# Returning expert rows to their tokens by 0/1 products instead of a scatter and a read-back

## The reference

```
combine = g_onehot[..., None] * within[..., None, :] * g_w[..., None, None]   # two entries per token
hg  = einsum('sd,edf->sef', xs, w_gate)
hu  = einsum('sd,edf->sef', xs, w_up)
act = silu(hg) * hu * cw[..., None]
out = einsum('sef,efd->sd', act, w_down)
x   = x + g_f[:, None, :] * out
```

## Time and profile before

| | us |
|---|---|
| median of 3 runs | 1921.35 (1921.19 to 1922.46) |
| span of the profiled execution | 1919.5 |
| PE / DVE / ACT / POOL busy | 1742.8 / 1019.5 / 553.4 / 859.7 |
| expert stage, first gather to last addition to the residual | 485 to 772.5 |

### The profile page before, as it was taken

One profiled execution on the slowest core, in us unless ns is written; L12 is line 12 of the kernel. 1 busy time (PEld: TensorE's weight loads), 2 busy tenths in 40 slices (PEclk: granted clock), 3 DMA queues, 4 the chain that ended last, 5 costly groups with the idle time before them and its releaser, 6 DMA issues.

```text
span 1919.5 us, 27022 instructions
## 1 busy us (share of the span) xinstructions
PE 1742.8 (91%) x10840; PEld 1275.8 (66%) x10840; DVE 1019.5 (53%) x1386; ACT 553.4 (29%) x995; POOL 859.7 (45%) x408
## 2 busy tenths in 40 slices
PE   6999888999797775899989899999999899999997
PEld 4868658875332322588767667777777678888885
DVE  6586896654111002496867958665798832222112
ACT  4341461533222222334434334564100120100000
POOL 0421235441110113045252342424898968787884
PEclk8999989999798897999999999999999999999999
DMA  8821223445799997222222121213457223233331
GB/s 303 318 89 55 66 87 115 158 155 186 270 410 409 409 408 283 82 88 88 66 66 66 58 74 56 72 61 121 143 208 257 99 77 99 89 98 95 103 99 66
DMA packets 81765, 290.53 MB, mean 151 GB/s; under 512 B 11120, under 2 KB 11120, under 8 KB 81008
## 3 DMA queue, kind: packets, MB, share of 16 engines
q1 hardware_dynamic: 74880, 271.54, 40.1%
q10 hardware_dynamic: 2160, 8.91, 1.2%
q0 software_dynamic: 4608, 8.40, 1.2%
HBM read 282.25 MB, written 14.94 MB: 155 GB/s over the span
## 4 chain that ended last, share of the span: by engine, by line
PE 51%; issue 18%; POOL 13%; DMA 6%; DVE 6%; ACT 3%; SPq 2%; POOLq 0%; DVEq 0%; ACTq 0%
PE bank L2715 50%; POOL lo_ring L2658 6%; DMA arena<-weights_dram 5%; POOL hi_ring L2686 4%; POOL lo_ring L2688 3%; SPq L2992 2%; PE bank L2719 1%; DVE arena L2305 1%; DMA arena<-h_dram,slot_table 0%; DVE hT L2618 0%; DMA late<-mod_weights_dram 0%; DVE arena L2376 0%; DMA xT<-x_dram 0%; DVE arena L1154 0%; DVE xT L1169 0%
## 5 line engine op out<-in xcount | busy, mean ns | idle before, releaser
L2715 PE MATMUL bank<-h_lo,hi_ring 128*128 128x512 f32 x648 | 257.1, 397 | 0.0
L2658 POOL TENSOR_TENSOR lo_ring<-ring,hi_ring 128x1024 fp32r<-128x1024 f32 x52 | 149.9, 2886 | 234.9 <-ACT hi_ring L2652 234.9
L2715 PE MATMUL bank<-arena 64*64 64x64 f32 (+4 forms) x1880 | 207.7, 366 | 49.0 <-DMA arena<-weights_dram 39.5
L2715 PE MATMUL bank<-mix_h_hi,lo_ring 128*128 128x512 f32 x576 | 230.7, 401 | 0.0
L2688 POOL TENSOR_TENSOR lo_ring<-ring,hi_ring 128x1024 fp32r<-128x1024 f32 x77 | 208.7, 2711 | 6.0
L2715 PEld LDWEIGHTS bank<-arena 64*64 64x64 f32 (+2 forms) x1880 | 107.0, 155 | 134.5 <-issue 121.5
L2686 POOL TENSOR_TENSOR hi_ring<-ring,col 128x1024 fp32r<-128x1024 f32 x77 | 159.2, 2068 | 55.7 <-PE bank L2715 55.3
L2715 PE MATMUL bank<-mix_h_hi,hi_ring 128*128 128x512 f32 x416 | 168.3, 405 | 16.9 <-POOL lo_ring L2658 6.4
L2305 DVE SCALAR_TENSOR_TENSOR arena<-bank,col,arena 128x511 f32<-128x511 f32 (+14 forms) x240 | 156.5, 723 | 0.0
L2715 PEld LDWEIGHTS bank<-h_lo,hi_ring 128*128 128x128 f32 x648 | 123.2, 190 | 27.9
L2715 PE MATMUL bank<-ffn_h_hi,lo_ring 128*128 128x512 f32 x352 | 139.2, 395 | 0.0
(11 more groups left out here) (445 smaller groups left out, 3911.6 us busy)
## 6 DMA issues: line engine op xcount, KB each, us to landing
ring<-weights_dram SPq DMA_DIRECT2D x230, 512.0 KB, 3.6
arena<-weights_dram SPq DMA_DIRECT2D x128, 512.0 KB, 13.4
arena<-mod_weights_dram SPq DMA_DIRECT2D x54, 512.0 KB, 4.7
late<-mod_weights_dram SPq DMA_DIRECT2D x42, 512.0 KB, 3.6
hT<-weights_dram SPq DMA_DIRECT2D x20, 512.0 KB, 15.5
late<-weights_dram SPq DMA_DIRECT2D x15, 512.0 KB, 14.7
arena<-y_dram ACTq DMA_DIRECT2D x8, 512.0 KB, 7.2
con<-weights_dram SPq DMA_DIRECT2D x5, 512.0 KB, 16.4
```

Source lines behind the costliest of these rows:

```text
L2658: pool.tensor_tensor(ring_r[:, u % RING, :], ring[:, u % RING, :], hi_unit(u).bitcast(F32), ALU.subtract).then_inc(S("split"), 1)
L2715: return pe.matmul(out, lhsT, rhs, start=start, stop=stop, skip_group_check=True)
```

## The change

It replaces the way back. Each slot gets two more numbers, its token's number and its weight (`slot_token`, `slot_weight`), made by a second set of small products from the table of picks. A slot that is empty has the number of no token.

- ScalarE writes the down result times the slot's weight in fp32r (`y_up`), VectorE the remainder (`y_low`).
- VectorE compares the slot's token number with the row of 512 token numbers: a 0/1 matrix of 128 slots by 512 tokens (`token_pick`).
- PE multiplies: for each of the 8 output tiles, `y_up` and `y_low` times `token_pick`, two fp32r products 128x512 into one bank. The result lies feature-major already.
- VectorE adds it, times the gate of the block, to the residual, tile by tile, for every pair (`add_rows`).

The scatter, `y_dram`, the read-back, the scaling and adding of choices and the 32 transposes are gone. The products of pair p-1 stand in four groups between the parts of gate_up(p+1), in banks 1 and 7 in turn. Bank 1 is no longer used by turn_rows, whose two halves both go through bank 0 and stand ahead of and between the two halves of down. The last two pairs use all eight banks and are added together at the end. The loops on ACT and DVE are written out. Of the five early upper parts, one now stands ahead of the last weighted rows, two behind them, one behind the squares and one behind the norm's halves.

```diff
-            def turn_rows(p):
+            def turn_rows(p, i):
...
-                    pe.wait_ge(*at_count("expert_in", p * 2))
+                if p == 1:
+                    pe.wait_ge(*at_count("expert_in", i + 1))
+                elif p:
+                    pe.wait_ge(*at_count("expert_in", p * 2 + i))
+                into = bank[i if p < 2 else 0]
...
+            def to_tokens(p, n, start=True, stop=True):
+
+                into = token_bank(p, n)
+                if n % 4 == 0:
+                    pe.wait_ge(*at_count("token_pick", p + 1))
+                    pe.wait_ge(*at_count("y_low", p * 2 + n // 4 + 1))
+                if p < PAIRS - 2 and p * KD + n > 1:
+                    pe.wait_ge(*at_count("x_added", p * KD + n - 1))
+                d = slice(n * P, n * P + P)
+                mm(into[:, :], y_up_r[:, p % 2, d], token_pick_r[:, p % 2, :], start, False)
+                last = mm(into[:, :], y_low_r[:, p % 2, d], token_pick_r[:, p % 2, :], False, stop)
+                if stop:
+                    last.then_inc(S("in_tokens"), 1)
...
+            for p in range(PAIRS):
+                if p + 1 < PAIRS:
+                    pe.wait_ge(*at_count("expert_in", p * 2 + 4))
+                    for j in range(4):
+                        gate_up_part(p + 1, j)
+                        if p:
+                            to_tokens(p - 1, 2 * j)
+                            to_tokens(p - 1, 2 * j + 1)
+                turn_act(p)
+                if p + 2 < PAIRS:
+                    turn_rows(p + 2, 0)
...
+                if p == PAIRS - 1:
+                    pe.wait_ge(*at_count("x_added", KD * (PAIRS - 2)))
+                    pe.wait_ge(*at_count("y_low", 2 * (PAIRS - 1)))
+                    for n in (0, 1, 2, 3, 6, 7):
+                        to_tokens(p - 1, n, True, False)
+                down_half(p, w, 0)
                 if p + 2 < PAIRS:
-                    turn_rows(p + 2)
-                down(p)
...
+                    turn_rows(p + 2, 1)
+                down_half(p, w, 1)
+            for n in range(KD):
+                pe.wait_ge(*at_count("y_low", 2 * PAIRS - 1 + n // 4))
+                if n in (4, 5):
+                    to_tokens(PAIRS - 2, n, True, False)
+                to_tokens(PAIRS - 1, n, False, True)
...
+            def rows_up(p):
...
+                    act.activation(y_up_r[:, p % 2, d], bank[4 + half][:, :], ACT.Identity, bias=column("zero"),
+                                   scale=slot_weight[:, p:p + 1]).then_inc(S("y_up"), 1)
...
+                dve.tensor_scalar(token_pick_r[:, p % 2, :], token_ids, slot_token[:, p:p + 1], None, ALU.is_equal).then_inc(S("token_pick"), 1)
...
+                    dve.scalar_tensor_tensor(y_low_r[:, p % 2, d], bank[4 + half][:, :], slot_weight[:, p:p + 1], y_up_r[:, p % 2, d].bitcast(F32),
+                                             ALU.mult, ALU.subtract).then_inc(S("y_low"), 1)
...
-                pool.indirect_dma_start(out=y_d, out_offset=bass.IndirectOffsetOnAxis(ap=slot_table[:, PAIRS + p:PAIRS + p + 1], axis=0),
-                                        in_=y_rows[:, p % 2, :], in_offset=None, bounds_check=2 * T - 1, oob_is_err=False).then_inc(S(f"y_stored{p % 2}"), 16)
```

More of the change, by code:

```diff
@@ L243 @@
     "act_turned": ("combine_turned", 0),
-    "sparse_y": ("y_lo", 7),
+    "y_low": ("y_lo", 7),
     "expert_in": ("y_hi", 8),
@@ L250 @@
     "two_heads": ("totals", 1),
-    "y_picked": ("gates_lo", 1),
 }
@@ L1377, in pe_moe @@
             last.then_inc(S("ranks_done"), 1)
-            out = take(("slots",), ("slots", 1))
+            out = take(("slots",), ("slot_weights", 1))
             pe.wait_ge(*at_count("picks_ranked", 1))
@@ L1382, in pe_moe @@
                     half = slice(CAP_E * i, CAP_E * i + CAP_E)
-                    last = mm(out[half, 0:2 * PAIRS].rearrange("p (v e) -> p v e", v=2), slot_of[:, n, :],
-                              slot_value[:, :, n, i:NE:2], n == 0, n == 2 * TT - 1)
+                    last = mm(out[half, 0:PAIRS], slot_of[:, n, :], slot_value[:, 0, n, i:NE:2], n == 0, n == 2 * TT - 1)
             last.then_inc(S("slots_done"), 1)
+            pe.wait_ge(*at_count("pick_weights", 1))
+            for n in range(2 * TT):
+                for i in range(2):
+                    half = slice(CAP_E * i, CAP_E * i + CAP_E)
+                    last = mm(out[half, PAIRS:2 * PAIRS], slot_of[:, n, :], slot_value[:, 1, n, i:NE:2], n == 0, n == 2 * TT - 1)
+            last.then_inc(S("slot_weights_done"), 1)
             u0 = at["moe_units"] = unit[0]
@@ L1651, in gate_up @@
[L1651 to L1663 removed]
+            def turn_rows(p, i):
+                if i == 0:
+                    pe.wait_ge(*at_count(f"gathered{p % 2}", p // 2 * 16 + 16))
+                if p == 1:
[3 more added lines that the diff above has]
+                into = bank[i if p < 2 else 0]
+                for n in range(4):
+                    last = flip(into[:, n * P:n * P + P], rows_in[:, p % 2, (4 * i + n) * P:(4 * i + n + 1) * P])
+                last.then_inc(S("rows_turned"), 1)
@@ new lines, in gate_up_part @@
+            def gate_up_part(p, j):
+                w = [weights(p, 2 * j + e) for e in range(2)]
+                for kk in range(2):
+                    k = 2 * j + kk
+                    for e in range(2):
+                        slots = slice(CAP_E * e, CAP_E * e + CAP_E)
+                        last = mm(bank[2 + 4 * (p % 2)][slots, :], rows_t[:, p % 2, k * P + CAP_E * e:k * P + CAP_E * e + CAP_E],
+                                  w[e][:, kk * 512:kk * 512 + 512], k == 0, k == KD - 1)
+                        if kk:
+                            last.then_inc(S("unit_done"), 1)
@@ L1670, in turn_act, with down_half @@
                 last.then_inc(S("act_turned"), 1)
-            def down(p):
+            def down_half(p, w, half):
+                if p:
+                    pe.wait_ge(*at_count("y_low", p * 2 + (half - 1)))
+                for i in range(4):
+                    f, e = divmod(i, 2)
+                    last = mm(bank[4 + half][CAP_E * e:CAP_E * e + CAP_E, :], sparse_act[:, f * P + CAP_E * e:f * P + CAP_E * e + CAP_E],
+                              w[i][:, half * 512:half * 512 + 512], f == 0, f == 1)
+                    if half:
+                        last.then_inc(S("unit_done"), 1)
+                if not half:
+                    last.then_inc(S("sparse_down"), 1)
@@ L1724, in act_out @@
                 act.activation(sparse_act, bank[3][:, 0:2 * P], ACT.Copy).then_inc(S("sparse_act"), 1)
-            rows_out(0, 0)
-            rows_out(1, 1)
-            silu(0, 0, 8)
-            with act.Fori(0, PAIRS // 2 - 1) as i:
-                for j in range(2):
-                    p = i * 2 + j
-                    act_out(p)
-                    silu(p + 1, 1 - j, i * (2 * PAIR_UNITS) + (16 + PAIR_UNITS * j))
-                    rows_out(p + 2, j)
-            act_out(PAIRS - 2)
@@ new lines, in act_sparse @@
+            act.wait_ge(*at_count("slot_weights", 1))
+            rows_out(0)
+            rows_out(1)
+            silu(0)
+            for p in range(PAIRS):
+                act_out(p)
+                if p + 1 < PAIRS:
+                    silu(p + 1)
+                else:
+                    act.preload_act_table_set(LN_EXP)
+                if p + 2 < PAIRS:
+                    rows_out(p + 2)
+                if p == PAIRS - 1:
+                    act.wait_ge(*at_count("unit_done", MIX_FIRST - 4))
+                    act_upper(act, MIX_FIRST)
+                rows_up(p)
```

194 lines of the change are left out of this document (79 added, 115 removed).

## The result

The changed kernel takes 1928.7 us (median of 6 runs, 1924.6 to 1931.6) against 1921.3 us for the kernel before (6 runs on the same chip). The ratio is 1.0031 with a 95% interval of 1.0018 to 1.0044. So it is slower by 0.3 to 0.4%, some 6 to 7 us, which is more than the 0.2% that a measurement can tell. I had forecast 1923.0, within a range of 1909 to 1935. The profiled execution spans 1929.4 us, that of before 1919.5.

What follows compares the result with a forecast made beforehand. Before, the matrix engine bound first, then DMA; after, the matrix engine at 17.01 us a pair. Profiled span 1919.5 + 1.7 later + 1.85 around it = 1923.0 us; eight-in-ten range 1909 to 1935.

Steps and rivals of the forecast that it cites:

- The sign: Whole kernel against the one before: faster (below 1917.5 us) 0.30, same 0.33, slower (above 1925.2 us) 0.37.
- What binds the stage: Expert stage: the matrix engine binds at 17.0 us a pair, borders included, DMA below it; 1923.0 us, chance 0.50.
- hidden borders (1904): Expert stage: the matrix engine's queue largely hides tile-form borders; 15.65 us a pair, 1904 us in total; chance 0.24.
- DMA as the bound: Expert stage: DMA stays the bound at 16.25 us a pair, 1912.5 us in total; chance 0.04.
- the late hand-over chain: Before first products: row copies, weighted rows, remainder late, matrix engine waits; 0.65 us a pair, 1932 us; chance 0.22.
- The period: Matrix engine per pair: 11.43 existing work + 3.70 products + 1.62 borders + 0.26 copy stall = 17.01 us.
- The estimate of what DMA allows (15.65 us): Expert stage: DMA alone, without the scatters, allows 15.65 us a pair, from 16.25 us less 0.6 us.
- rival 4: Expert stage: DMA keeps binding at 16.25 us a pair, only if borders are hidden too; 1912.5 us, chance 0.04.
- The start of the stage: Before the first pair: slot-weight products and copies run beside the gather at no cost; stage taken 0.7 us earlier.
- The other half of the step: Pair 1's turns wait for only half of pair 0's row copies; gate/up starts some 0.9 us earlier, taken as 0.7.
- The tail: Stage end, from the start of pair 14's turns (S) to the squares' sum's reader: 24.4 us; last product at S+17.5.
- the mark: Start of the squares' sum's reader after the stage, the comparison point: 777.5 us forecast against 775.83, 1.7 us later.

Runs made afterwards that it cites:

- experiments 4: Changed kernel with the second half of each pair's row turns moved into a token-product group: 1923.62 us, ratio 1.0002 to the kernel before.
- Experiment 6: Changed kernel, all edits combined: slot-weight products behind branch, second turns in group, group over copy wait, third token bank, groups of three; 1914.14 us, ratio 0.9951.
- experiment 3: Changed kernel with the remainder's product left out, one product per output tile in place of two: 1901.4 us in one run.
- experiment 2: Changed kernel with the slot weights' products and copies moved behind the overflow branch: 1926.23 us, ratio 1.0025 to the kernel before.

## Why the prediction came out as it did

The sign that I gave the largest chance (slower, 0.37) came true, the time was 5.7 us above the forecast, and the range held it. The sign is in part luck. The parts that I gave add up to 0.31 faster, 0.35 same and 0.34 slower, so by them "same" came first. And of the 7 us by which the kernel is slower, the forecast had 1.7; what made the rest is below. Point by point, by the steps of the prediction:

- **What binds the stage: right.** TensorE's own sum, in every pair, with DMA below it. The granted clock is 1.00 from 509 us to the end of the stage (0.66 between 507 and 509), where I had said from 505. Of the rivals, hidden borders (1904) fall by experiments 4 and 6; DMA as the bound falls by the list of waits, which has none for weights, and by experiment 3; the late hand-over chain does not occur: no wait for VectorE in front of a group in the body.
- **The period: 17.01 forecast, 17.11 measured.** The half-width steps and the turns are as read; the products go at 0.231, as the rows at other places had it. What lies beside them was put at 1.88 us (1.62 + 0.26) and is 1.98. A group's border there and back is 0.36, not 0.34, three times; the second turns' visit cost 0.34, not 0.25. What is left, 0.56 us, is the fourth group's way in, the way out of the turns behind it and the stall at the activation's copy, where I had 0.20 + 0.15 + 0.26 = 0.61. Over 14 pairs the 0.10 is 1.3 us.
- **The estimate of what DMA allows (15.65 us): wrong,** and without effect, since 17.11 is above 16.1 too. It was made from 16.25 us a pair, which is a miscount: that eight scatters fall in a window of 130 us does not make eight periods of it. The first and the last of them in the timeline of the kernel before:
```profile
606.36 1.01 POOL L1805 DMA_INDIRECT y_dram<-arena,slot_table  x1 [14.68 <-DVE arena L1763]
725.28 0.99 POOL L1805 DMA_INDIRECT y_dram<-arena,slot_table  x1 [15.44 <-DVE arena L1763]
```
  These are seven periods in 118.9 us, so 17.0 us a pair. Less the 0.6 of the scatter that is 16.4, near the 16.1 that bytes over rate give; the stock lets single pairs go below either. The sum of the forecast did not use the figure, the price of rival 4 and the view of what was to be won did: of the phase bound by DMA, at 17.0 us a pair before, nothing was left to win for a kernel that takes 17.1.
- **The start of the stage: the step that failed.** "The second set of weights for slots runs beside the gather: nothing." Its products do lie beside the gather. But they stand ahead of the branch, and what TensorE spends behind the branch without a wait came 3.5 us later against the gather and stuck out by 2.2 us over before (8.70 to 10.91, experiment 2; 2.6 by the means of two traces each). I had looked for work to cover, and not for the idle time put down to issue. The other half of the step was right: the turns of pair 1 start after half of the copies, and gate/up starts 5.21 us after the first turn, not 6.08 (0.9 less, as forecast). What is left of it at the first copy is 0.6 us in the first pair of traces and 0.2 in the second, 0.7 forecast. The kernels of the experiments scatter there from 20.05 to 21.50.
- **The tail: 24.4 us forecast, 25.0 measured** from the turns of pair 14 (759.63) to the mark (784.64). The wait for the second remainder is there with 1.60 us, the last products end at 777.5 = S + 17.9, 17.5 forecast.
- **The rest of the miss lies ahead of the stage.** At the mark, in the first trace of each kernel, the miss is 8.8 - 1.7 = 7.1 us: 2.2 at the branch, 1.3 in the period, 0.6 in the tail, 0.1 in the first turns. The other 2.8 lie ahead of the gather: 1.8 up to the last addition before the router, 1.0 from there to the gather's issue (20.82 against 19.85; before took 21.12 in its other trace). Whether code ahead of the stage is slower in the kernel after by more than chance is open: its last addition came between 462.98 and 471.03 in eight traces of its kin, at 465.09 and 465.37 in two of before.

The windows behind the mark in the kernel after, which answer to the earlier trace rows:
```profile
785.00:788.00 3.00, 0.00 (x0) 0.00 (x0) 1.72 (x3) 2.02 (x4) 0.00 (x0) 1.00 0.01 3
788.00:792.00 4.00, 3.41 (x9) 2.34 (x10) 4.00 (x7) 1.93 (x4) 0.00 (x0) 0.57 0.00 0
```
The granted clock is 0.57 behind the wait of four us, where the earlier trace rows has 0.53: alike in both, as I had assumed. The table has 1143.7 and 1146.5 us behind the mark for before, 1144.8 and 1146.8 for after.

Where did the expected gain of such a change go? Before, TensorE stood idle or waited for 51 us in the 14 pairs (214.7 - 14 x 11.69), and the tail was 20.2 us longer. The change pays for this with 3.70 us of products in each pair, and with borders and stalls that rose from 0.25 to 1.98 us a pair (17.11 - 11.43 - 3.70). Together these are 5.42 us a pair, 76 in 14 pairs, against the 51. In the nine pairs bound by DMA the two cancel (+1.5 us). The five pairs ahead of them, four of which ran at TensorE's own 11.7 us, had almost nothing to pay with (+23.3 us). Experiment 6 gets 15.3 us of the stage back without a product less, 14.6 of them by the 1.04 us of each pair.

The borders come first from the rows: a change from half-width work to full width and back was put at 0.25 to 0.34 us and measured 0.34 to 0.36. The Trainium skill (TensorEngine Tiling (Array Packing), section Key Properties) has it that a change of the tiling mode drains the engine. The trace agrees as far as each change between the 128*64 and the 128*128 form costs time, and the change from products to turns within 128*128 costs none. That the engine drains is not seen in a trace. The page gives no price, and the runs here give one.

## What to carry to other kernels

When work moves onto the engine that has the gaps, count how often it will change its form of tile there, and not only the work: fewer and larger groups, placed next to work of the same form or where the engine waits anyway, turned +0.3% into -0.5% with the same products, 2.2 us of it by the place of the slot weights' products. A transfer that is "the bound" in a window binds only once its stock is spent: take bytes over rate from the first request to the last landing, and not for one pair. A gain from a phase that another engine binds is worth its own period there: count it from event to event, not by events in a window. And work that is hidden beside a transfer is not free if it stands ahead of a branch behind which the profile shows idle time put down to issue: it pushes that along.

## What the hardware showed that I had not expected

- Behind the branch TensorE stands still for 7.4 us (combined kernel) to 8.5 us (kernel after), in all eight traces of the changed kernels, with nothing to wait for that the profile shows. The profile calls it issue. The DMA engines are full for most of it (410 to 412 GB/s from 488 to 496 us in the kernel after).
- Filling a wait of 0.23 us that stood just ahead of a change from full to half width gave back 0.34 us.
- Between products and turns of the same 128*128 form there is no border (0.23 us from the last product to the first turn).
- TensorE ran its own sum to within 0.02 us in 13 pairs running (17.11, 16.77, 16.07 us), and in nine at 14.21, beside DMA at 370 to 409 GB/s: no sign of contention between the two.
